# Expert stage of a two-layer decoder step: part of the down products moved around the last transposes, and the next expert's first gate product moved ahead of the last scatter

## What is computed

```python
def _swiglu(h, wg, wu, wd):
    return (jax.nn.silu(h @ wg) * (h @ wu)) @ wd

def _moe(h, rw, rb, wg, wu, wd):
    logits = (h @ rw + rb).astype(F32)
    top_v, top_i = lax.top_k(logits, TOP_K)
    probs = jax.nn.softmax(top_v, axis=-1)
    comb = jnp.sum(jax.nn.one_hot(top_i, N_EXPERTS, dtype=F32) * probs[..., None], axis=-2)
    ...
    for e in range(N_EXPERTS):
        out = out + comb[..., e:e + 1] * _swiglu(h, wg[e], wu[e], wd[e])
    return out
```

## Time and profile before

| what | value |
|---|---|
| median of 3 runs | 1450.38 us (1448.49 to 1454.55) |
| the profiled execution's own time | 1451.43 us |
| its span in the trace | 1449.7 us, so 1.7 us lie around it |
| mean granted clock of TensorE | 0.944 of full speed |
| chain that ended last, by engine | TensorE 72%, VectorE 17% |
| expert stage in the trace | about 961 to 1426 us |

### The profile page before, as it was taken

The page is one execution under the profiler, slowest core; times in us unless marked ns, Lnnn a source line. Parts: engine busy times, 40 slices in busy tenths (PEclk is TensorE's granted clock), DMA queues, the critical chain, the costliest instruction groups (busy, mean ns, idle before and its releaser), DMA issues.

```text
span 1449.7 us, 22628 instructions
## 1 busy us (share of the span) xinstructions
PE 1304.0 (90%) x8970; PEld 1268.1 (87%) x8970; DVE 984.6 (68%) x1298; ACT 679.6 (47%) x779; POOL 63.4 (4%) x117
## 2 busy tenths in 40 slices
PE   4785789999999999898869999999999999999895
PEld 4774789999999999798769989999999999999894
DVE  6799943466655555489882445658888888788773
ACT  4254122344443243345522334566566667566562
POOL 2000500100000000000210200000000000000000
PEclk9897799999999999999989999979999999999998
DMA  6320583445645346132474534548778787887860
GB/s 215 106 87 30 121 171 106 134 149 176 204 158 164 123 153 204 58 106 88 104 128 134 145 115 145 218 160 308 288 282 320 286 319 293 290 320 270 303 228 38
DMA packets 47466, 262.77 MB, mean 181 GB/s; under 512 B 6048, under 2 KB 6624, under 8 KB 34832
## 3 DMA queue, kind: packets, MB, share of 16 engines
q1 hardware_dynamic: 42048, 243.55, 48.0%
q0 software_dynamic: 4752, 15.37, 5.7%
q10 hardware_dynamic: 576, 2.62, 0.5%
HBM read 255.89 MB, written 5.62 MB: 180 GB/s over the span
## 4 chain that ended last, share of the span: by engine, by line
PE 72%; DVE 17%; issue 4%; DMA 3%; ACT 3%; DVEq 0%; ACTq 0%; SPq 0%
PE bank L1856 21%; PE bank L1858 21%; PE bank L1857 21%; DMA raw<-w_in_in 3%; DVE w_lo L1101 2%; DVE mw_lo L1107 1%; PE bank L1868 1%; PE bank L1847 1%; PE bank L2101 1%; ACT w_hi L781 1%; ACT mw_hi L788 1%; PE bank L2064 1%; PE bank L1974 1%; PE s_bank L1974 1%; PE s_bank L2138 1%
## 5 line engine op out<-in xcount | busy, mean ns | idle before, releaser
L1107 DVE TENSOR_TENSOR mw_lo<-mraw,mw_hi 128x2816 fp32r<-128x2816 f32 x96 | 295.8, 3088 | 64.9 <-ACT mw_hi L788 63.8
L1856 PE MATMUL bank<-hn_hi,w_hi 128*128 128x320 f32 x656 | 220.1, 335 | 54.6 <-DVE w_lo L1101 41.9
L788 ACT ACTIVATE mw_hi<-mraw 128x2816 fp32r<-128x2816 f32 x96 | 244.9, 2551 | 27.5 <-PE bank L1858 27.5
L1101 DVE TENSOR_TENSOR w_lo<-raw,w_hi 128x1024 fp32r<-128x1024 f32 x128 | 154.3, 1223 | 92.7 <-ACT w_hi L781 89.6
L1857 PE MATMUL bank<-hn_lo,w_hi 128*128 128x320 f32 x656 | 214.3, 327 | 0.0
L1858 PE MATMUL bank<-hn_hi,w_lo 128*128 128x320 f32 x656 | 213.6, 326 | 0.0
L1856 PEld LDWEIGHTS bank<-hn_hi,w_hi 128*128 128x128 f32 x656 | 133.6, 204 | 62.5 <-DVE w_lo L1101 46.5
L1856 PE MATMUL bank<-mw_hi,x_hi 128*128 128x352 f32 x512 | 168.7, 330 | 1.9 <-DVE x_lo L1717 1.9
L1858 PE MATMUL bank<-mw_hi,x_lo 128*128 128x352 f32 x512 | 166.2, 325 | 0.0
L1857 PE MATMUL bank<-mw_lo,x_hi 128*128 128x352 f32 x512 | 165.8, 324 | 0.0
L781 ACT ACTIVATE w_hi<-raw 128x1024 fp32r<-128x1024 f32 x128 | 132.9, 1052 | 69.1 <-PE bank L1858 47.7
(11 more groups left out here) (452 smaller groups left out, 2722.6 us busy)
## 6 DMA issues: line engine op xcount, KB each, us to landing
mraw<-w_moe_in SPq DMA_DIRECT2D x96, 1408.0 KB, 7.1
raw<-w_in_in SPq DMA_DIRECT2D x88, 512.0 KB, 4.2
uraw<-w_gu_in SPq DMA_DIRECT2D x44, 512.0 KB, 3.8
raw<-w_br_in SPq DMA_DIRECT2D x24, 512.0 KB, 4.6
uraw<-w_dn_in SPq DMA_DIRECT2D x16, 704.0 KB, 4.1
raw<-w_wo_in SPq DMA_DIRECT2D x16, 512.0 KB, 3.6
toep<-k_scratch POOLq DMA_DIRECT2D x16, 256.0 KB, 11.7
pl<-pl_in POOLq DMA_DIRECT2D x2, 1840.0 KB, 8.2
```

What stands on the lines that cost most here:

```text
L788: act.activation(mw_hi[c % MSPLIT][:, :], mraw[slot][:, :], ACT.Copy).then_inc(hi_ready, 1)
L1101: dve.tensor_tensor(w_lo[g % SPLIT][:, :], raw[slot][:, :], w_hi[g % SPLIT][:, :].bitcast(F32), ALU.subtract).then_inc(lo_ready, 1)
L1107: dve.tensor_tensor(mw_lo[c % MSPLIT][:, :], mraw[c % MRAW][:, :], mw_hi[c % MSPLIT][:, :].bitcast(F32), ALU.subtract).then_inc(lo_ready, 1)
L1856: pe.matmul(out, w_h[k], x_h[k], start=start and k == 0, stop=False)
```

## The change

It moves instructions in the queues of TensorE and VectorE; it adds and removes none. ScalarE's and SyncE's queues stay as they are.

- `down(q)` becomes `down(q, k0, k1)`, for tiles k0 to k1. Tiles 0 to 7 of down(0) now stand ahead of T3, behind a wait for T2's copies; behind T3 come tiles 0 to 3 of down(1), then the wait for T3's copies and the rest of both.
- `projected` moves out of the item, and the next expert's chunk 0 is run between scatter(2) and scatter(3). In the second of a pair it waits for the fourth gather's `x_lo`. The very first one stands ahead of the loop.
- On VectorE, the low part of the next expert's chunk 2 moves ahead of the last two of the four adds.

```diff
--- before.py
+++ after.py
@@ -1733,6 +1733,7 @@
                     low(NEXP * r, 1)
                 for q in range(4):
                     tokens_low(of_round(r, q), small_bank[(1 + q) % 4], r, q, q)
+                low(0 if isinstance(r, int) else NEXP * r, 2)
 
                 def item(p, e, u, it, last):
                     def product(b):
@@ -1794,9 +1795,9 @@
                             if e and not last:
                                 tokens_low(*small_no(r, p, e, "G0"), r, 4 + 4 * p, 0)
                             hidden_low(3)
-                        if c + 2 < N_CHUNK:
+                        if 0 < c < N_CHUNK - 2:
                             low(it, c + 2)
-                        elif not last:
+                        elif c and not last:
                             low(it + 1, c + 2 - N_CHUNK)
                     if e and not last:
                         tokens_low(*small_no(r, p, e, "G2"), r, 6 + 4 * p, 2)
@@ -1804,6 +1805,8 @@
                     result_low(3)
                     scattered(4)
                     scattered(5)
+                    if not last:
+                        low(it + 1, 2)
                     scattered(6)
                     scattered(7)
 
@@ -2103,6 +2106,17 @@
                                            start=i == 0 and b == 0, stop=i == 1 and b == 2)
                 mm.then_inc(small_full, 1)
 
+            def projected(it, e, c):
+                b, out = c // 2, wide_bank[c % 4][:, 0:BLK]
+                pe.wait_ge(lo_ready, parted(it, c))
+
+                pe.wait_ge(v_free, up_done(it, b - 2) if b >= 2 else down_done(it - 1, c))
+                w_h, w_l = (w[c % MSPLIT][:, :].rearrange("p (k n) -> p k n", k=KD) for w in (mw_hi, mw_lo))
+                for k0 in (0, 4):
+                    ks = range(k0, k0 + 4)
+                    product3(out, [x_hi[:, k, e] for k in ks], [x_lo[k // 2][:, k % 2, e] for k in ks], [w_h[:, k] for k in ks],
+                             [w_l[:, k] for k in ks], v_full if k0 else None, start=not k0, stop=bool(k0))
+
             def round_(r):
                 pe.wait_ge(disp_ready, 1 + N_PAIRS * r)
                 if isinstance(r, int):
@@ -2112,6 +2126,7 @@
                     gather(4 if isinstance(r, int) else of_round(r, q), small_bank[(1 + q) % 4], q)
                 pe.wait_ge(small_free, of_round(r, 4))
                 pe.sem_inc(round_begun, 1)
+                projected(0 if isinstance(r, int) else NEXP * r, 0, 0)
 
                 def item(p, e, u, it, last):
                     def small_take(name):
@@ -2119,17 +2134,6 @@
 
                         pe.wait_ge(small_free, no - 2 if name == "PS" else no - 3)
                         return out
-
...
                     def transposed(b):
                         out = small_take(f"T{b}")
@@ -2138,18 +2142,15 @@
                             mm = pe.transpose(out[:, SLOTS * j:SLOTS * j + SLOTS], hid[:, P * k:P * k + P], ident[:, :])
                         mm.then_inc(small_full, 1)
 
-                    def down(q):
-                        pe.wait_ge(lo_ready, parted(it, 8 + q))
-                        pe.wait_ge(v_free, up_done(it, 2 + q // 2))
+                    def down(q, k0, k1):
+                        if k0 == 0:
+                            pe.wait_ge(lo_ready, parted(it, 8 + q))
+                            pe.wait_ge(v_free, up_done(it, 2 + q // 2))
                         w_h, w_l = (w[(8 + q) % MSPLIT][:, :].rearrange("p (k n) -> p k n", k=FT) for w in (mw_hi, mw_lo))
-                        last_tiles = BLK_TILES[3][0]
-                        for k0, k1 in ((0, last_tiles), (last_tiles, FT)):
-                            if q == 0:
-                                pe.wait_ge(small_free, small_no(r, p, e, "T3" if k0 else "T2")[0] + 1)
-                            ks = range(k0, k1)
-                            product3(wide_bank[q][:, 0:QTR], [ht_hi[:, k] for k in ks], [ht_lo[:, k] for k in ks],
-                                     [w_h[:, k] for k in ks], [w_l[:, k] for k in ks], v_full if k0 else None,
-                                     start=not k0, stop=bool(k0))
+                        ks = range(k0, k1)
+                        product3(wide_bank[q][:, 0:QTR], [ht_hi[:, k] for k in ks], [ht_lo[:, k] for k in ks],
+                                 [w_h[:, k] for k in ks], [w_l[:, k] for k in ks], v_full if k1 == FT else None,
+                                 start=not k0, stop=k1 == FT)
 
                     def scatter(q):
 
@@ -2161,9 +2162,9 @@
                                 .then_inc(small_full, 1)
 
                     for b in range(4):
-                        projected(2 * b)
                         if b:
-                            projected(2 * b + 1)
+                            projected(it, e, 2 * b)
+                            projected(it, e, 2 * b + 1)
                             transposed(b - 1)
                             continue
 
@@ -2179,23 +2180,32 @@
                             mm = pe.matmul(out[:, TOKS[b] + p0:TOKS[b] + P], disp[:, b, e], ident_r[:, p0:P],
                                            start=True, stop=True)
                         mm.then_inc(small_full, 1)
-                        projected(1)
+                        projected(it, e, 1)
                     if e and not last:
                         pe.wait_ge(disp_ready, p + (2 + N_PAIRS * r))
                         gather(*small_no(r, p, e, "G0"), 0)
+                    last_tiles = BLK_TILES[3][0]
+                    pe.wait_ge(small_free, small_no(r, p, e, "T2")[0] + 1)
+                    down(0, 0, last_tiles)
                     transposed(3)
-                    down(0)
-                    down(1)
+                    down(1, 0, 4)
+                    pe.wait_ge(small_free, small_no(r, p, e, "T3")[0] + 1)
+                    down(0, last_tiles, FT)
+                    down(1, 4, FT)
                     scatter(0)
                     if e and not last:
                         gather(*small_no(r, p, e, "G1"), 1)
-                    down(2)
+                    down(2, 0, FT)
                     scatter(1)
                     if e and not last:
                         gather(*small_no(r, p, e, "G2"), 2)
                         gather(*small_no(r, p, e, "G3"), 3)
-                    down(3)
+                    down(3, 0, FT)
                     scatter(2)
+                    if not last:
+                        if e:
+                            pe.wait_ge(small_free, small_no(r, p, e, "G3")[0] + 1)
+                        projected(it + 1, 1 - e, 0)
                     scatter(3)
 
                 items(pe, r, item)
```

More of the change, by code:

```diff
@@ L2121, in small_take @@
                         return out
-                    def projected(c):
-                        b, out = c // 2, wide_bank[c % 4][:, 0:BLK]
-                        pe.wait_ge(lo_ready, parted(it, c))
-                        pe.wait_ge(v_free, up_done(it, b - 2) if b >= 2 else down_done(it - 1, c))
-                        w_h, w_l = (w[c % MSPLIT][:, :].rearrange("p (k n) -> p k n", k=KD) for w in (mw_hi, mw_lo))
-                        for k0 in (0, 4):
-                            ks = range(k0, k0 + 4)
-                            product3(out, [x_hi[:, k, e] for k in ks], [x_lo[k // 2][:, k % 2, e] for k in ks], [w_h[:, k] for k in ks],
-                                     [w_l[:, k] for k in ks], v_full if k0 else None, start=not k0, stop=bool(k0))
                     def transposed(b):
```

## The result

The changed kernel takes 1460.57 us in the median, against 1454.00 for the kernel before in the same comparison: ratio 1.0042, 95% interval 1.0025 to 1.0060. It is slower, and outside the range that was forecast. The kernel before is itself 3.6 us longer here than the 1450.38 on which the forecast stood; that is a part of the 14.1 us between 1446.5 and 1460.57, and without it the time would still be outside.

The account below looks back on a forecast made before the run. TensorE, busy 90%, was taken as the bound, with its waits for VectorE to be covered. Terms of -4.4, -0.4, +0.3 and +0.5 gave -4.0 us: 1447.4 from an execution of 1451.43, as a median 1446.5; range 1440.5 to 1453.

Parts of the forecast that it names:

- Then 3.82, 0.58 and 0.92: projected(1) at 1201.28: Second of a pair: gate product, scatter(3), then PS and S; projected(1) at 1201.28 instead of 1201.57, -0.29 us.
- The 0.92 for PS and S: TensorE behind scatter(3): PS and S take 0.92 us before projected(1) starts.
- The wait at T3 changes its name and grows: TensorE's wait for `hid` becomes one for `ht_lo` at the first down matmul, 0.46 us longer, some 19 us in all.
- `mw_lo` was forecast at 0.7 four times: Firsts of a pair: projected(4) asks for chunk 4 before VectorE has it ready and waits 0.7 us, four times.
- Five drops of the clock at T3: Ahead of down(0): five drops of TensorE's clock instead of four, +1.3 us.
- The sum was -4.0: Whole change: scatter nets -4.4 and -0.4, T3 of the eighth expert +0.3, T3's copies +0.5, together -4.0 us.
- T2 to the first down matmul: T2's transposes to down(0): the start stays as before, 1117.38, since VectorE still takes `hidden_low(2)` behind `product(3)`.
- T3 and its copies: TensorE at the down products: T3 on its path costs 0.28 us per expert, the wait for its copies 0.06.
- Chunk 10's low part: VectorE behind T3: chunk 10 starts 4.5 us behind the first down matmul instead of 1.2.
- The clock was taken as nothing: TensorE's clock: one drop goes at the scatter, one comes ahead of down(0); together nothing, bounds -6.3 and +4 us.
- A: Rival: down(0) finds its `ht_lo` ready, so waits at T3 and scatter both go; -32.5, 1418 us; chance 0.04.
- C: Rival: VectorE becomes the bound, its late low parts delay projected(4) in seven experts; 1457.7 us; chance 0.08.

Follow-up runs that it names:

- e3_again: The changed kernel once more, unaltered: 1461.52 us, ratio to the kernel before 1.0084.
- e9_same_chip: The changed kernel once more, unaltered, to stand beside two other runs on one chip: 1458.16 us, ratio to the kernel before 1.0051.
- e6_before80: The kernel before, no work moved, with 80 more instructions at TensorE's begin: 1464.73 us, ratio to the kernel before 1.0078.
- e11_straight: The changed kernel with TensorE's three turns of the pair loop written out, no jump on TensorE: 1449.83 us, ratio to the kernel before 0.9988.
- e5_pad207: The changed kernel with 207 more TensorE instructions, waits long met, ahead of its first gate products: 1454.88 us, ratio to the kernel before 1.0017.
- e2_down_only: The kernel before with the down part of the change alone, gate product and chunk 2's low part at their old places: 1466.45 us, ratio 1.0116.
- e4_late9: The changed kernel with VectorE's low part of chunk 9 behind product(3) and hidden_low(2): 1436.46 us, ratio to the kernel before 0.9902.
- e1_scat_only: The kernel before with the scatter part of the change alone, down products as before: 1436.99 us, ratio to the kernel before 0.9907.
- e12_late9_straight: The changed kernel with VectorE's low part of chunk 9 late and TensorE's turns written out: 1429.11 us, ratio to the kernel before 0.9846.
- e10_pad60: The changed kernel with 60 more instructions at TensorE's begin: 1464.93 us, ratio to the kernel before 1.0104.

## Why the prediction was wrong

**The step that failed.** "Then 3.82, 0.58 and 0.92: projected(1) at 1201.28", for what follows a second of a pair. The 0.92 for PS and S took for granted that TensorE goes from scatter(3) to PS without a break. At the two places where the loop jumps back this is so only if its program is still held. In both traced executions of usual length (e3_again and e9_same_chip, 30 packets) it isn't, in the short one of the result (12 packets) it is; by their times most of the others had the reload, but they weren't traced. It costs 3.5 us of stall and 1.5 of slower products at each jump, and e3_again's stage is 8.7 us longer than that of the result's profile, more than twice the 4.0 that the change was to bring. At the place to which the change's 49 instructions moved it, the loop is held in some executions and not in others. No term of the sum and no rival had this; e6_before80 shows it without any of the change's reordering, e11_straight takes it away with all of it in place.

**What was right.** The wait at T3 changes its name and grows: some 19 us forecast, 20.2 measured, with VectorE's order as the cause. `ym_lo` falls to the last expert's 0.5. `x_lo` was forecast at 0.4 three times and is 0.45. `mw_lo` was forecast at 0.7 four times and is 0.45. Five drops of the clock at T3 were forecast, and the result's profile has five.

**What was luck.** The sum was -4.0, and the stage gives -2.8 in the result's profile, -3.1 in e5_pad207 and -5.9 in e11_straight, where the turns written out also drop the loop's own counting (58 instructions a turn). But 1.6 us of each stand at the stage's begin, from the first gate product to the first projected(1), where all these kernels run the same matmuls; before, then changed:

```profile
961.61:968.02 6.41, 6.41 (x34) 6.41 (x34) 3.09 (x1) 3.33 (x3) 0.00 (x0) 0.73 0.26 109
```

```profile
963.37:968.22 4.85, 4.85 (x33) 4.85 (x34) 1.97 (x1) 3.56 (x3) 0.00 (x0) 1.00 0.17 72
```

The profile of before has a drop of the clock there that no term spoke of; e2_down_only, which has this product at its old place, has none (4.85 us, clock 1.00). So only 1.2 of the 2.8 us answer to the forecast's 4.0. The medians of the two kernels whose profiles show no reload are +3.1 (e5_pad207) and -0.9 (e11_straight) against their own runs of before: by time the change itself shows no gain.

**What was mis-sized.** The missing 2.8 us are small errors of the walk, nearly all to the same side. T2 to the first down matmul was to stay "as before" and takes 3.61 us in six experts of eight; before it was 3.42 in five. T3 and its copies cost 0.38 (8.35 us from the first down matmul to scatter(0) in the fourth expert, 7.97 before), not 0.34. With a drop that stretch takes 9.8 to 9.9 us, so a drop costs 1.5, not 1.3. In the seconds of a pair the gate product comes 1.21 us behind scatter(2), 0.8 earlier than before, not 1.0. Chunk 10's low part comes 6.0 us behind the first down matmul in the third expert, not 4.5: the clock fell there.

The clock was taken as nothing, with five drops at T3; the traces of the changed kernel show five (the result), four (e3_again) and three (e9_same_chip) there, and e5_pad207 four. But the longer executions of e5_pad207 have a lower mean granted clock (0.943 to 0.946, at 1452.7 to 1457.5 us) than the shorter (0.946 to 0.950, at 1449.6 to 1449.9). More drops would fit; no longer one was traced, and this stays open.

**The rivals.** A's premise, `ht_lo` ready for the first down matmul, needed VectorE's queue changed, as the prediction argued; e4_late9 changes it, and the wait falls by two thirds. C did not come: `mw_lo` stays at 1.8 us. The forecast left out the halves: by e1_scat_only the scatter part alone would have been worth 12.7 us, and the down part gives 8.5 us of stage back, of which the idle rows hold 6.8 (4.6 more at T3, 1.4 of `x_lo`, 0.8 more of `mw_lo`). I added their delays into one net per expert and did not see that one half was a loss.

**Open.** e1_scat_only's loop lies at the same place as the changed kernel's, and its profile has it held (12 packets), as the result's profile has. So near the edge something besides the place decides; what, was not tried. Nor was it traced why the medians of e5_pad207 and e11_straight lie 5 to 6 us above what their stages give.

## What to carry to other kernels

Code ahead of a hardware loop moves the loop within its engine's program; where a long loop jumps back, look at the instruction queue's packets in the trace, and if packets come in every turn, write the turns out or shift the loop by some instructions. Before covering a wait on one engine with other work, see whether the engine waited for has something in its queue that could stand later: here that one move gave 20 us or more (e12_late9_straight against e11_straight, e4_late9 against e3_again), and the cover alone lost 11 us of stage (e2_down_only). Where the executions of one kernel spread by more than the change is worth, profile a short one and a long one: the profile of the short one alone would have shown a change that worked.

## What the runs showed of the hardware

- TensorE runs a loop of 1635 instructions (768 matmuls, 768 weight loads, 99 others) without reading it again: no q8 packet in the second and third turn of the result's profile, 12 in the stage. Shifted by 31 or 60 instructions beyond the changed kernel's place, it reads the loop again in every turn, 30 packets in the stage, and stands 4.8 us (e6_before80) or 3.9 us (e10_pad60, in two parts) at each jump; at the changed kernel's own place it is 3.3 to 3.7 where the loop is read again. The page of the Trainium skill named above has the stall, but speaks of a window of two blocks outside which a jump misses; here more than six blocks' worth of loop stayed held, and the trace decides. The same section gives TensorE room for 2048 instructions, which the held loop agrees with.
- Reading straight on costs nothing that shows: 24 packets and no wait in e11_straight.
- The profile can name a releaser for such a stall that had ended earlier (VectorE's add in e3_again, by 0.7 us); in e6_before80 and e10_pad60 such stalls read "issue".
- The clock's drops in the stage go with the waits ahead of them: with waits at T3 up to 1.2 us there is none in 440 us (e12_late9_straight), of the five waits of 2.9 to 3.1 us at T3 in a trace of the changed kernel three to five have one, and the same wait of 3.11 us in the third expert came with one (the result) and without (e3_again).
